# Order of two groups of TensorE work in the attention stage: outputs of a piece, then the transposes of the piece two ahead

## What is computed

```
# forgetting head
s = q @ k.T;  bias = cum[q] - cum[k];  p = softmax(where(causal, s + bias, -inf));  o = p @ v
# dilated head: three windows (128,1), (512,4), (2048,16), each a softmax with its log-sum,
# mixed with softmax(lse); the kernel folds them into one softmax with log(count of windows) added
```

## Time and profile before

| | |
|---|---|
| median of 3 runs | 1308.87 us |
| the profiled execution | 1310.72 us, span 1308.6 us |
| TensorE (PE) busy | 1242.4 us, 95% |
| VectorE (DVE) busy | 753.9 us, 58% |
| ScalarE (ACT) busy | 490.7 us, 37% |
| GpSimd (POOL) busy | 413.5 us, 32% |
| attention stage | 296 to 502 us of the span, mean granted TensorE clock 0.98 of full |
| TensorE, VectorE, ScalarE busy in those 206 us | 187.1, 158.7, 152.4 us |

### The profile page before, as it was taken

The page is one execution under the profiler, slowest core; times in us unless marked ns, Lnnn a source line. Parts: engine busy times, 40 slices in busy tenths (PEclk is TensorE's granted clock), DMA queues, the critical chain, the costliest instruction groups (busy, mean ns, idle before and its releaser), DMA issues.

```text
span 1308.6 us, 18571 instructions
## 1 busy us (share of the span) xinstructions
PE 1242.4 (95%) x6504; PEld 1053.9 (81%) x6504; DVE 753.9 (58%) x1351; ACT 490.7 (37%) x940; POOL 413.5 (32%) x349
## 2 busy tenths in 40 slices
PE   6999999998999996999999999999999989999996
PEld 4899888877888885888788888888888868888885
DVE  7461655246787777476685655565565462333357
ACT  7323221246777775244243333333333322202212
POOL 5039532132555520000623323332332232202200
PEclk8899999998999998999999999999999999999998
DMA  5123343257555622124212212221221254330302
GB/s 202 50 81 80 115 116 145 97 148 212 145 130 129 144 57 65 49 65 129 97 49 97 97 50 94 96 77 67 96 96 58 87 216 202 129 128 2 129 26 103
DMA packets 45780, 135.85 MB, mean 104 GB/s; under 512 B 17126, under 2 KB 17174, under 8 KB 43020
## 3 DMA queue, kind: packets, MB, share of 16 engines
q1 hardware_dynamic: 40140, 117.37, 25.6%
q0 software_dynamic: 5296, 16.87, 6.8%
q10 hardware_dynamic: 288, 0.85, 0.2%
HBM read 98.81 MB, written 35.68 MB: 103 GB/s over the span
## 4 chain that ended last, share of the span: by engine, by line
PE 86%; DVE 6%; issue 3%; ACT 3%; DMA 1%; DVEq 0%; POOL 0%; ACTq 0%; SPq 0%; POOLq 0%
PE ps L2262 18%; PE ps L2241 9%; PE ps L2243 9%; PE ps L2242 9%; PE ps L2189 7%; PE ps L2100 3%; PE ps L488 3%; PE ps L489 3%; PE ps L490 3%; PE ps L2084 2%; PE ps L1983 2%; PE ps L1984 2%; PE ps L1985 2%; PE ps L2214 2%; PE ps L2216 2%
## 5 line engine op out<-in xcount | busy, mean ns | idle before, releaser
L1147 DVE TENSOR_TENSOR ev<-ps,ev 128x512 f32<-128x512 f32 x133 | 90.2, 690 | 116.1 <-PE ps L2243 116.1
L1147 DVE TENSOR_TENSOR z<-ps,z 128x512 f32<-128x512 f32 x80 | 51.5, 686 | 123.6 <-PE ps L2262 123.1
L2241 PE MATMUL ps<-t_hi,s_hi 128*128 128x512 f32 x304 | 118.3, 389 | 0.0
L2242 PE MATMUL ps<-t_lo,s_hi 128*128 128x512 f32 x304 | 118.3, 389 | 0.0
L2243 PE MATMUL ps<-t_hi,s_lo 128*128 128x512 f32 x304 | 118.3, 389 | 0.0
L1147 DVE TENSOR_TENSOR ptl<-ps,pth 128x512 fp32r<-128x512 f32 (+1 forms) x120 | 76.2, 636 | 32.4 <-ACT pth L959 30.2
L1063 ACT ACTIVATE s_hi<-s_sum 128x512 fp32r<-128x512 f32 x72 | 45.6, 633 | 131.0 <-PE ps L2243 131.0
L2241 PE MATMUL ps<-op_hi,s_hi 128*128 128x512 f32 x228 | 88.7, 389 | 0.0
L2242 PE MATMUL ps<-ol,s_hi 128*128 128x512 f32 x228 | 88.7, 389 | 0.0
L2243 PE MATMUL ps<-op_hi,s_lo 128*128 128x512 f32 x228 | 88.7, 389 | 0.0
L949 ACT ACTIVATE pr<-ps,nm 128x896 f32<-128x896 f32 (+3 forms) x96 | 71.2, 742 | 31.6 <-DVE nm L1418 30.8
(11 more groups left out here) (331 smaller groups left out, 3284.9 us busy)
## 6 DMA issues: line engine op xcount, KB each, us to landing
hid_scratch<-hf SPq DMA_DIRECT2D x22, 512.0 KB, 2.9
w_raw<-w_stream SPq DMA_DIRECT2D x18, 512.0 KB, 3.9
raw_b<-w_stream SPq DMA_DIRECT2D x18, 512.0 KB, 4.9
qk_scratch<-qk_hi SPq DMA_DIRECT2D x12, 512.0 KB, 2.6
qk_scratch<-qk_lo SPq DMA_DIRECT2D x12, 512.0 KB, 2.9
qa<-qk_scratch POOLq DMA_DIRECT2D x24, 256.0 KB, 4.2
ks<-qk_scratch POOLq DMA_DIRECT2D x24, 256.0 KB, 5.6
hb_raw<-hid_scratch SPq DMA_DIRECT2D x3, 2048.0 KB, 7.5
```

The source lines that it names most:

```text
L1147: return dve.tensor_tensor(out, a, b, op)
L2241: pe.matmul(out, s_hi[:, j, k], x_hi[:, k, :], start=k == 0, stop=False)
L2242: pe.matmul(out, s_hi[:, j, k], x_lo[:, k, :], start=False, stop=False)
```

## The change

In the unit's list of TensorE, `outputs` of piece (g,b) is issued ahead of `transposed` of the piece two ahead, where it was issued behind it. Nothing else is changed: the number and the kinds of the instructions, the waits of each function and the lists of the other engines stay as they are. The first two pieces are transposed ahead of the units, as before.

```diff
@@ -2132,10 +2132,10 @@
                 for b in range(max(g + 1, QB)):
                     if b < QB and ahead_:
                         scores(*ahead_, b)
+                    if b <= g:
+                        outputs(i, j, g, b)
                     if b <= g and on[b]:
                         transposed(*on[b])
-                    if b <= g:
-                        outputs(i, j, g, b)
                     if b == min(g, 1) and prev:
                         y_back(*prev)
```

## The result

The changed kernel took 1326.85 us, the median of 4 runs (1321.27 to 1329.07), against 1308.86 us for the kernel before beside it: ratio 1.0124, 95% interval 1.0099 to 1.0149. The direction was forecast, the size was not: +18.0 us where +8.4 was predicted, outside the range. Repeated later with 8 runs, the same kernel took 1320.34 us (1317.44 to 1326.50) against 1308.87 us (27 runs, 1305.93 to 1319.49): ratio 1.0076, interval 1.0049 to 1.0104. The two measurements differ by more than one would like, and the first question is why.

The account below looks back on a forecast made before the run. A loop through TensorE, VectorE and ScalarE, none full, was taken to bound the kernel. Division waits in 11 heads (7.85 us) plus ends (0.2 and 0.4) gave +8.4 on 1308.87: 1317.3 us, range 1313 to 1321.

Parts of the forecast that it names:

- The mechanism: At (3,0), outputs wait for unit 2's division with transposes of (3,2) queued behind: +0.65 us per forgetting head, +0.79 per dilated.
- what shifts the division itself: Late transposes of (1,0) delay unit 0's division, then transposes of (3,1) and unit 2's division: 0.12 us a head.
- the step from the division to the outputs: At (3,0), from the division's end on VectorE to the waiting outputs' start on TensorE: 0.05 us.
- The rest of a head: From the transposes of (2,0) onward, the swaps add 0; up to 0.1 us a head if (1,0)'s high part slips.
- the `y_done` wait at (1,0): Outputs of (1,0) wait for unit 0's division, ending before the exponential the next transposes need: cost 0.
- The ends: First head between 0 and 0.7 us, taken 0.2; last head's late transposes between 0 and 1.0, taken 0.4.
- The weight loads: Waiting outputs load weights only when the wait ends, group 0.58 us; loading during it would give 0.48, sum 1.1 lower.
- The range: Whole kernel's time forecast at 1313 to 1321 us.
- 2.6 us can be told from no change: A measurement of the whole kernel tells about 0.2% (2.6 us) from no change.
- Faster: Rival: TensorE's order sets the pace, so filling two gaps a head gives up to -10.4 us, 1298.5; chance 0.05.
- 0.14 us a head at best: Gain from filling the stalls before the transposes of (3,0) and (2,0): 0.14 us a head at best.
- Slower by more: Rival: the exponential of unit 3, r = 1, also slips 0.3 us a head: +12.0 us, 1320.9; chance 0.10.

Follow-up runs that it names:

- (3,0) alone: Outputs ahead of transposes only at piece (3,0), all else as in the kernel before: heads 17.67 / 17.75 us (forgetting / dilated), ratio 1.0058 to before.
- all but (3,0): Outputs ahead of transposes at every piece except (3,0), against the kernel before: heads 17.32 / 17.34 us (forgetting / dilated), ratio 1.0058.
- for (1,0): Outputs ahead of transposes only at piece (1,0), against the kernel before: heads 16.71 / 16.77 us, ratio 0.9977; run again, 16.72 / 16.77 us, 0.9982.
- for both: Outputs ahead of transposes only at (1,0) and (3,3), against the kernel before: heads 16.64 / 16.70 us, ratio 0.9966.

## Why the prediction was wrong

**The mechanism was right.** The waits moved as forecast: the transposes' wait for the exponential went without a gain of its own, the outputs wait for the division, and the transposes of (3,2) stand behind. (3,0) alone costs 0.66 / 0.78 us a head, against 0.65 and 0.79 in the prediction, and its 8.2 us on the stage against 7.85.

**But that agreement is partly luck, and two terms of the sum were too small.** The stage grew by 11.7 us where 8.4 was forecast. Of the 3.3 us between them 2.4 stand in the ten heads from the second to the eleventh (9.6 us, forecast 7.2), 0.7 in the first head and 0.1 in the last. In the ten heads the step that failed is the path from the exponential over the two divisions to the transposes of (3,2): "what shifts the division itself", set to 0.12, and the step from the division to the outputs, set to 0.05.

*The shift, 0.12.* The prediction had seen that the transposes of (1,0) come 0.48 later, that the division of unit 0 follows and that the outputs of (1,0) wait for it. It put the high part of (1,0) at 0.30 late, where the changed kernel shows 0.28 in dilated but 0.40 in forgetting heads, and took 0.05 for the step behind the division, where it is 0.13 (450.82 to 450.95). The transposes of (3,0) then come 0.29 / 0.34 us late behind the exponential, not 0.22, and those of (3,1) 0.21 / 0.28 late, not 0.12 (dilated / forgetting heads, averages over the fourth to the tenth head). So 0.09 / 0.16 us a head were missing.

*The step, 0.05.* The start of the outputs behind a division was taken from the last head, where the waits are against constants. In the loop it is 0.23 us in the changed kernel: 0.18 us a head were missing, and the transposes of (3,2) start 0.80 us behind the division, not 0.65. In (3,0) alone this 0.18 us stood in for the 0.12 of the shift that is not in that kernel; hence the luck above.

*The rest of a head, 0.* In the changed kernel this was nearly right: behind the row maximum of unit 2, r = 1, a head gives back 0.03 / 0.08 us. But the prediction called the `y_done` wait at (1,0) harmless, as it would "end before the exponential the next transposes wait for". In the kernel with all but (3,0) the wait did end about then (outputs at 426.94, end of the exponential 427.04), but the group behind it takes 0.57, and the transposes of (3,0) came at 427.51, 0.47 behind the exponential's end where it had been 0.14.

**The ends.** In the last head, which has a wait at (3,0) too, 1.05 was forecast (0.65 and 0.4); the distance from its first transposes to its last grew by 1.16 us. For the first head 0.2 was taken, and it grew by 0.94 in the first profile and by 1.80 in the second. The mean clock over it was 0.86 before and 0.85 and 0.82 in these, so how much of this belongs to the order of the groups is open.

**The weight loads.** The forecast went by the row and not by what the Trainium skill (TensorE: Matmul & The Clock Gate, "Step-by-step: what each phase is for") says of weight loads pulled ahead of running matmuls. The trace after agrees with the row: the load of the waiting outputs began with their first matmul and not in the 0.85 us before, and the second matmul followed 0.22 us behind the first.

```profile
455.05 0.19 PEld L2119 LDWEIGHTS ps<-pth,vs 128*128 128x128 f32 x1 [0.85 <-DVE ptl L1147]
455.06 0.38 PE L2119 MATMUL ps<-pth,vs 128*128 128x256 f32 x1 [0.71 <-DVE ya L1147]
455.28 0.28 PE L2120 MATMUL ps<-ptl,vs 128*128 128x256 f32 x1
```

Outputs that stand right behind transposes have nearly the same step without a wait, 0.19 us at 372.09 before, so 0.22 us is not the price of the wait alone.

**The range.** Of the 18.0 us measured first, the attention stage explains 11.7. That alone would have been 1320.6, at the range's end, and the second measurement, 1320.34, lies there too. The rest goes with the run-to-run swing of the clock, which moves this kernel's time by up to 13 us (1305.93 to 1319.49 in 27 runs) and which three runs of the kernel before, within 2.4 us, did not show. The statement that 2.6 us can be told from no change was too confident for a few runs.

**The rivals.** "Faster" held that filling the gaps gives up to 10.4 us: it gives 2.3 to 3.2 for (1,0), at most 4.6 for both, if nothing else is moved; the first head, whose clock differs from run to run, is in these figures. "0.14 us a head at best" was too low for it: 0.20 to 0.30, because with the transposes of (3,1) left ahead of the outputs of (1,1) they follow those of (3,0) 0.39 us sooner (0.81 against 1.20). "Slower by more" had nearly the stage's figure, 12.0 against 11.7, but not its cause: it had the long exponential of unit 3 slip by 0.3 us a head, and that exponential starts 1.33 us behind the start of its row maximum, 1.32 to 1.33 before. So the change held a gain and a loss. Most of the gain needs one swap of ten; the loss came with others, (3,0) above all.

## What to carry to other kernels

When a group of work is moved on an in-order engine, list every wait of the group that now stands in front, not only the one both have in common, and follow each delay round the loop to the next wait of the same kind: the wait for the division at (3,0) was covered here to within some 0.03 us, and passed on any delay ahead of it. Move one place at a time and read the length of a period from the trace, which repeated to 0.02 us where whole runs swung by 13; and test pairs too, as a delay that one swap makes can be taken up or kept by the next. Fill a gap only with work that is ready, and only if nothing that feeds another engine is queued behind it.

## What the runs showed of the hardware that was not expected

In the changed kernel the step from the division's end to the waiting outputs of (3,0) was 0.05 to 0.06 us in the three written-out heads that have this wait, whose waits are against constants, and 0.23 us in the eight heads of the loop, with a second wait behind the first. With that second wait put first it was 0.06 in the looped dilated heads and 0.15 in the forgetting ones, and 0.14 to 0.15 in the written-out heads. That the working out of the second wait's value is what takes the time is argued, not shown, and the written-out heads, which became slower, do not fit it alone.

The same stretch of small matmuls from 160 to 200 us ran at full clock in some executions and at a mean of 0.75 to 0.78 from 180 to 200 us in others, in kernels that are identical there. Attention began at 303.9 to 307.2 us in the four profiles with the lower clock and at 297.5 to 300.2 us in the ten others. In both kinds of execution TensorE had stood idle for some 0.85 us and then ran the same small matmuls (L2022, L2023) without a gap; in the changed kernel's first profile their step went from 0.22 to 0.43 us at 176, in the kernel before it stayed at 0.22. What tips it is open.
